# A trunk layer on one Trainium2 core: VectorE's two adds of y moved forward in each half of the expert stage

## The reference, cut to what matters

```python
g = jax.nn.softmax(best_s, axis=-1)
act = jax.nn.gelu(jnp.einsum('thkd,td->thk', u[idx], hb), approximate=False)
return jnp.einsum('thk,thkd->td', g * act, v[idx])
```

## Time and profile before

| | us |
|---|---|
| median of 3 runs | 3334.67 |
| lowest, highest | 3320.79, 3336.86 |
| profiled execution | 3342.92 |
| its span | 3341.1 |
| PE busy in the span | 3136.2 (94%) |
| DVE busy | 2363.6 (71%) |
| POOL busy | 1673.7 (50%) |
| ACT busy | 1015.7 (30%) |

### The profile page before, as it was taken

The page is one execution under the profiler, slowest core; times in us unless marked ns, Lnnn a source line. Parts: engine busy times, 40 slices in busy tenths (PEclk is TensorE's granted clock), DMA queues, the critical chain, the costliest instruction groups (busy, mean ns, idle before and its releaser), DMA issues. The chain is left out here.

```text
span 3341.1 us, 44529 instructions
## 1 busy us (share of the span) xinstructions
PE 3136.2 (94%) x14956; PEld 2541.8 (76%) x14956; DVE 2363.6 (71%) x4287; ACT 1015.7 (30%) x1182; POOL 1673.7 (50%) x1329
## 2 busy tenths in 40 slices
PE   6999588997999999999998799999999999999997
PEld 3889465686888887888887677777777877777776
DVE  4612465463688888666664688888888888888888
ACT  2110134432333323444444222222222222222221
POOL 2000224413433323333332777777777777777774
PEclk7999678998999999999999899999999999999999
DMA  5610000022332323445444898898898999999897
GB/s 208 212 64 26 10 14 26 1 91 91 111 107 88 107 79 123 159 160 214 163 163 189 272 298 298 288 297 287 293 299 302 304 301 300 298 306 300 292 306 283
DMA packets 325786, 645.75 MB, mean 193 GB/s; under 512 B 169264, under 2 KB 170560, under 8 KB 322752
## 3 DMA queue, kind: packets, MB, share of 16 engines
q1 hardware_dynamic: 233280, 338.08, 31.7%
q0 software_dynamic: 91264, 272.96, 23.1%
q10 hardware_dynamic: 1152, 33.55, 2.4%
HBM read 568.98 MB, written 75.50 MB: 193 GB/s over the span
## 5 line engine op out<-in xcount | busy, mean ns | idle before, releaser
L2152 DVE SCALAR_TENSOR_TENSOR total<-ex_ring,ex_pick,total 128x1024 f32<-128x1024 f32 x512 | 650.7, 1291 | 225.9 <-DMA ex_ring<-peer_v_dram,sp_row 217.6
L2009 POOL DMA_INDIRECT ex_pick<-act_scratch,sp_place x512 | 576.7, 1126 | 175.7 <-issue 155.7
L2014 POOL DMA_INDIRECT ex_ring<-peer_v_dram,sp_row x512 | 578.1, 1129 | 156.1 <-issue 129.9
L2042 PE MATMUL ex_dots<-h_hi_b,ex_uhi 128*128 128x512 f32 x1024 | 401.3, 392 | 23.7 <-ACT ex_uhi L2084 14.4
L2042 PE MATMUL ex_dots<-h_lo_b,ex_uhi 128*128 128x512 f32 x1024 | 400.7, 391 | 0.0
L1891 DVE TENSOR_SCALAR gm_b_hot<-gm_iota,second_T,gate_T 128x128 f32<-128x128 f32 x512 | 257.7, 571 | 170.1 <-PE gm_prod L1835 167.4
L2101 ACT ACTIVATE ex_whi<-ex_dots 128x512 fp32r<-128x512 f32 x128 | 76.8, 600 | 925.0 <-DVE ex_dots L2132 925.0
L1415 POOL TENSOR_TENSOR ga_ulo<-ga_u,ga_uhi 128x1024 fp32r<-128x1024 f32 x72 | 173.2, 2407 | 341.8 <-ACT ga_uhi L1409 341.6
L2045 PE MATMUL ex_dots<-h_hi_b,ex_ulo 128*128 128x512 f32 x1024 | 252.8, 389 | 0.0
L2052 PE MATMUL ex_y<-ex_vhi,ex_whi 128*128 128x512 f32 x512 | 216.3, 422 | 33.7 <-DVE total L2123 27.9
L2042 PEld LDWEIGHTS ex_dots<-h_hi_b,ex_uhi 128*128 128x128 f32 x1024 | 193.9, 189 | 64.9 <-ACT ex_uhi L2084 14.9
(11 more groups left out here) (302 smaller groups left out, 6758.4 us busy)
## 6 DMA issues: line engine op xcount, KB each, us to landing
ex_u<-peer_u_dram SPq DMA_DIRECT2D x128, 512.0 KB, 5.5
ex_v<-peer_v_dram SPq DMA_DIRECT2D x128, 512.0 KB, 8.0
ga_u<-peer_u_dram SPq DMA_DIRECT2D x72, 512.0 KB, 3.6
gate_scratch<-gm_out ACTq DMA_DIRECT2D x8, 4096.0 KB, 11.8
ex_g<-gate_scratch SPq DMA_DIRECT2D x128, 256.0 KB, 6.5
ra_u<-peer_u_dram SPq DMA_DIRECT2D x56, 512.0 KB, 3.6
act_scratch<-ga_act SPq DMA_DIRECT2D x72, 256.0 KB, 2.1
w_in_raw<-w_ada_dram SPq DMA_DIRECT2D x64, 256.0 KB, 3.7
```

What stands on the lines that cost most here:

```text
L2009: nc.gpsimd.indirect_dma_start(weights[:, i:i + 1], None, places, bass.IndirectOffsetOnAxis(ap=picks[:, i:i + 1], axis=0)).then_inc(pick_i ...
L2014: nc.gpsimd.indirect_dma_start(ring[:, i], None, rows, bass.IndirectOffsetOnAxis(ap=which[:, RING * s + i:RING * s + i + 1], axis=0)).then ...
L2042: nc.tensor.matmul(dots[:, c], uhi[:, c, kk], b[:, kk], start=kk == 0 and b is hi, stop=False)
L2152: nc.vector.scalar_tensor_tensor(total[:, t], ring[:, i], weights[:, bass.ds(PER * s + i, 1)], total[:, t], ALU.mult, ALU.add).then_inc(ro ...
```

## The change

In each chunk the first add of y moves from behind `low_weights` to between `weigh` and `low_u`, and the second from behind the fourth `add_row` to right behind `low_weights`. No instruction is added or removed, and the other engines' programs stay as they are.

```diff
                         low_v(s, b, c)
                         add_row(s, 4 * c + 1, opening)
                         weigh(s, c)
+                        if not opening:
+                            add(s - 1, 2 * c, first)
                         if not last or n + 2 < CH:
                             low_u(n + 2, c, False)
                         low_weights(s, b, c)
                         if not opening:
-                            add(s - 1, 2 * c, first)
+                            add(s - 1, 2 * c + 1, first)
                         add_row(s, 4 * c + 2, opening)
                         add_row(s, 4 * c + 3, opening)
-                        if not opening:
-                            add(s - 1, 2 * c + 1, first)
```

## The result

The changed kernel takes 3416.75 us (median of 4 runs, 3410.19 to 3427.97) against 3332.94 for the kernel before on the same chip: ratio 1.0261, 95% interval 1.0223 to 1.0299. It is slower by 84 us. The forecast was slower by 56, 3390 with a range up to 3410. The trace after is of an execution of 3427.97 us, 85 us above the traced one before.

A forecast was written before the change was run, and what follows sets the result against it. GpSimd's issues, held by VectorE's two-SBUF operations, were taken as the bound. Holds of 2.0 + 0.1 + 1.0 + 0.7 = 3.8 us a stage against 2.9 add 56 us over 62 stages: 3390 us, range 3285 to 3410.

The forecast's parts named there:

- GpSimd never waits: Expert stage before: gaps ahead of GpSimd's issues are 0.3 us at most, so GpSimd was taken to set the pace.
- the walk: Steps through VectorE's operations from r1 or r5, GpSimd starting 0.07 us behind, to find which operations hold its issues.
- 2.0 for ulo with r2: Two readers before ulo: GpSimd starts 0.12 us inside ulo or r2, held 1.0 per chunk, 2.0 us a stage.
- 1.0 for the vlo behind r4: GpSimd, in step, starts 0.07 us inside this vlo and is held; taken as 1.0 us a stage, bounds 0 and 1.03.
- r1 and r5 after VectorE's wait: Row adds that start at an arbitrary phase of GpSimd: holds of 0.7 us a stage, bounds 0.4 and 1.0.
- r0 and r4, 0.1: Row adds that lose the add of y before them: holds fall from 1.13 to 0.1 us a stage, bounds 0 to 0.7.
- Costed at nothing: Earlier adds of y, and ulo, wlo and SyncE's loads 0.6 us later, were claimed to cost or gain no time.
- (1): vlo lets GpSimd pass: holds 2.8 against 2.9, no change, 3318 to 3351, about 3332 us; chance 22%.
- rival 2: The pair of readers lets GpSimd through at ulo and r2: faster, 3267 us at TensorE's floor, half gives 3300; chance 18%.
- (3): TensorE is the bound and its waits for adds are the cost: up to 81 us less, not below 3267; chance 7%.
- rival 4: Holds of GpSimd's issues don't depend on the order of VectorE's operations: 3335 us; chance 3%.

The follow-up runs named there:

- read_all_again: Changed kernel plus three short PSUM readers a chunk on VectorE, in front of vlo, ulo and wlo, run a second time: 3268.28 us, ratio 0.9796.
- read_vlo_again: Changed kernel plus one short PSUM reader a chunk on VectorE, in front of vlo, run a second time: 3330.92 us, ratio 0.9979.
- first_only: Kernel before with only the first add of y moved, to behind weigh; the second stays behind the fourth row add: 3432.25 us, ratio 1.0294.

## Why the prediction was right or wrong

**The bound: right.** "GpSimd never waits" was the right row to start from, against the larger sums of waits of VectorE and TensorE. The pair without element gathers shows it: with eight issues less a stage both orders fall to TensorE's floor. The rule as I put it, that an engine with no wait sets the pace, is too strong: in `read_all_again` GpSimd has no gap over 0.31 us either, and TensorE is busy all the time.

**The mechanism: right, place by place.** Issues of 1.97 us beginning 0.12 or 0.13 us inside r2, and others 0.06 inside the vlo behind r4, stand in the trace as the walk had them. The forecast of 2.0 for ulo with r2 measured 2.06, that of 1.0 for the vlo behind r4 0.96. The choice at vlo ("I take 1.0, by the lengths") rested on two durations and no row of its own; it held in 56 of 60 stages. The twelve traces in which GpSimd issues both kinds on a chip like the first show how late a start passes. Behind a row add's start it passes up to 0.08 us (all but one of some 1500 issues), 0.09 is mixed, and the 490 between 0.10 and 0.20 are all held. Behind the start of vlo or ulo it passes up to 0.01 us, 0.02 and 0.03 are mixed, and the 539 between 0.04 and 0.20 are all held. The forecast had seen 0.07 pass and 0.12 held at a row add, and had put vlo's limit at about 0.03. What inside the engines makes that difference is not shown. The runs with one reader show both places to be causes: one short reader in front of the place makes its hold go, and time comes back (1.026 of before to 0.997 and 0.998). How much each hold was worth alone they don't give, since other places change with it: of the 1.43 us a stage that come back in `read_vlo_again`, 0.96 are vlo's.

**The size: wrong, and the range too low.** The step that failed is the sum of the holds after: two of its terms were too small. "r1 and r5 after VectorE's wait: I take 0.7" measured 1.01. I had reasoned that some of the 0.9 of now lay on other operations; it measured 0.85 on r1 and r5 alone. And it rose: 97 of the 120 r1 and r5 hold an issue after, 80 before, for 0.62 us each against 0.63. VectorE waits ahead of them hardly more often (106 times against 100) and somewhat longer (3.74 us a stage against 3.43). Why more of these starts fall where they hold stays open. "r0 and r4, 0.1" measured 0.33: VectorE now also waits ahead of r0, in 24 of 60 stages, and these give 0.19 of it. My walk had r0 follow without a wait; the 36 stages in which it does give 0.12.

The two terms are 0.54 us a stage too low together. The pair of ulo and r2 adds 0.06, and the base, 2.96 and not 2.9, takes 0.06 away. So the difference of the holds is 1.43 us a stage, not 0.9: 89 us over 62 stages, where 84 were measured and 56 forecast. The bounds of the single terms were good but for 0.01 us; the top of the range took them in part, and missed by 7 us.

**Costed at nothing: right, with one gap.** The pair without elements is the test: 3 us between the orders, within their intervals. TensorE's clock, 0.97 after, was in no term; what it cost in the changed kernel is not separated, but the halves of the change cost as much at 0.99.

**Rivals.** vlo does not let GpSimd pass (1). The pair of readers doesn't either (2), but its point of decision was well placed: 0.13 us more of PSUM reading in each gap frees ulo, r2 and r6, as rival 2 had it. That `read_all_again` gives 3268 beside its 3267 is TensorE's floor, reached in both; at vlo, which rival 2 had free, the holds stayed. TensorE as the bound (3) would have shown in the trace of after as time gained from the 63 us less of waits for adds; nothing was gained. That the order doesn't matter to GpSimd's issues (4) is contradicted by the issues held by r2 and vlo in the trace, and by the runs with one reader, which add 0.13 us a chunk and move the holds.

I read rival 4 off the inference in the Trainium skill ("SBUF — State Buffer", Who interferes with whom) that descriptor generation needs the write interface only. But an indirect DMA of this kernel also reads its row numbers from SBUF (`sp_row`, `sp_place` in the rows). The first sentence that I took from that section, on GpSimd ops that read SBUF, would then have the issues held, and the holds of up to 1.98 us agree with it. Which part of an issue is held, the reading of the numbers or the writing of descriptors, no run here separates.

## What to carry to other kernels

Look for the engine that never waits before you add up who waits longest, and check beside it that no other engine is busy all the time; then ask why its instructions are not all equally long, and set the long ones beside what the neighbour runs at that time. In this kernel GpSimd issues gathers with a period of 1.25 us, VectorE runs operations with two SBUF inputs beside them, and the length of the gaps between those operations counted to 0.1 us: 1.20 us of PSUM readers between them cost a hold in every chunk, and 1.33 us let GpSimd through at ulo, r2 and r6. Short readers that delay VectorE by 0.13 us were worth more than any reordering tried here. An order should be judged by the holds in its trace, not by how early each operation is done.

## What the runs showed of the hardware that was not expected

- **A double hold.** In `first_only` GpSimd, when it began 0.64 to 0.66 us inside r4, was held through r4 and vlo, 2.57 us in all (51 times); at 0.71 to 0.73 us inside it, in the kernel before, it came free at r4's end each time (59 times). The one issue of the kernel before that began at 0.65 was held through both, 2.58 us. Why these 0.05 us decide is open.
- **A memset is not a neutral filler.** One column moved the next start by 0.01 us; 192 columns delayed r2 and left GpSimd held for 2.06 us where 1.97 had been.
- **Chips differ.** The median of the kernel before was 3325 to 3336 us beside four sets of runs and 3551 us beside one, on another chip.
